# Moving half of the first pool half's window sums from the own blocks into attention's first units

## The chip, the cores and the metric

One Trainium2 chip, one program on all 8 cores. Each core owns 2,048 of the 16,384 positions and reads a halo of 2,048 positions before them; the cores do not talk to each other. The time of a run is device microseconds of its slowest core; a kernel's time is the median of its runs.

## The reference, cut to what matters

The layer runs a dilated window attention and a pooling mixer on one projection of the normalised input, merges them with gates, and follows with a SwiGLU network. The part that the change touches is the pooling mixer's trailing means:

```
for g, w in enumerate(POOL_WINDOWS):          # 2, 4, 8, 16; 64 channels each
    c = c0[:, :, g]                            # running sums of u
    ...
    z = (c[:, 1:] - lag) / cnt - ug[:, :, g]   # trailing mean minus the token
    outs.append(jnp.einsum('bsc,cd->bsd', z, w_mix[g]))
y = jnp.concatenate(outs, axis=-1) * scale
```

## The kernel before, in words

Every engine's program is written out in Python in the order in which that engine runs it; a semaphore wait stands ahead of an instruction that needs another engine's result. There is no planner: the place of a call in the code is its place in each engine's queue.

The program has five stages: the halo, the own blocks, attention, the merge with the gates and the output projection, and the feed-forward network. Two of them matter here.

**The own blocks** (loop over `b`, four blocks of 512 positions; inside it 12 chunks `n`). For each chunk TensorE makes a projection of q or k (eight matmuls, L449). In blocks 2 and 3 `rope_swap` turns it: VectorE multiplies the projection by the cosine and sine tables in one instruction (L548, out tile `t`), four small DMAs, two from SP's queue and two from ScalarE's, swap the rows of the sine part (`t2s<-t`), and GpSimd adds the two (L560). A projection lands in one of six PSUM banks and L548 sets the bank free. Four tiles `t` go round, so an L548 also waits for the L560 of four chunks earlier. After every third chunk a `u_unit` projects the pool's input and ScalarE copies it to `X` (L700).

The pool's 256 channels are two halves. The first half (`c0`, windows 2 and 4) is summed by `window_c0` in quarters of 512 positions, four VectorE pieces each: a pair sum (L721, `Y<-X`), a sum of pairs on the upper 64 partitions (L725, `Z<-Y`), and two means minus the token (L710, `zT<-Y` and `zT<-Z`, 64 partitions each). `c0_steps` is the list of these 16 pieces; before, one of them stands behind each of 16 consecutive L548, in the second half of block 2 and in block 3 up to chunk 9. The second half (`c1`, windows 8 and 16) is summed by `window_c1` in two halves of 1,024 positions, six pieces each (L732, L736, L739, L742, two L710).

**Attention** (loop over `u`, 48 units, group 2 in units 0 to 15, group 1 in 16 to 31, group 0 after them). In iteration `u` TensorE makes the scores of unit `u` (L852), projects v block `u`+3 (L569), and applies unit `u`-2 (L874, L879). ScalarE makes the exponential (L856, tile `PT`), copies the v block out of PSUM (L573) and, in group 2, copies the applied unit into `acc` (L894). VectorE multiplies by the mask (L861) and, from group 1 on, adds the applied unit to `acc` (L897). v blocks have two PSUM banks (6 and 7), and so have applied units (4 and 5, `o_ring`). Three v blocks are projected ahead of unit 0. In units 4, 8 and 12 VectorE copies the v block out in place of ScalarE (L575). At unit 1 VectorE's queue waits for the end of all rotary work (`ev_rope`, among it the last L560), at unit 2 ScalarE's. One `c1` piece stands in each of the units 1, 2, 3, 5, 6, 7, 9, 10, 11, 13, 14, 15. `pool_mix` (L811 on TensorE, L813 on ScalarE) maps the first half in units 17 to 20 and the second in 22 to 25. The first gate weights (`wgs`) are loaded once the last mean is there (`ev_wz[1]`) and used from unit 45 on.

Of the kernel before, what the change touches and what calls it, by code (L numbers as in the profile page):

```python
# [191 lines left out]
def build_program(taps=(), stop_after=None):  # L192
# [33 lines left out]
    pe, act, dve, pool, sp = P.pe, P.act, P.dve, P.pool, P.sp  # L226
# [251 lines left out]
    def k_dst(g, pr, e0, n):  # L478
        return kT[g][:, pr, e0 - KOFF[g]:e0 - KOFF[g] + n]
# [228 lines left out]
    def pool_mean(c, p0, S, X, t0, n, ev):  # L708
        p1 = p0 + 64
        ev = dve.op(lambda e: e.scalar_tensor_tensor(out=zT[p0:p1, c, t0:t0 + n], in0=S, scalar=invw[p0:p1, c:c + 1],  # L710
                                                     in1=X[p0:p1, t0 + 16:t0 + 16 + n], op0=ALU.mult, op1=ALU.subtract), waits=[ev])
        if t0 == 0:
            ev = dve.op(lambda e: e.tensor_tensor(out=S[:, 0:16], in0=S[:, 0:16], in1=invc[p0:p1, c, :], op=ALU.mult), waits=[ev])
            ev = dve.op(lambda e: e.tensor_tensor(out=zT[p0:p1, c, 0:16], in0=S[:, 0:16], in1=X[p0:p1, 16:32], op=ALU.subtract), waits=[ev])
        ev_wz[c] = ev

    def window_c0(q):
        X, t0, st = Xc[0], 512 * q, {}

        def y1():  # L720
            st[0] = dve.op(lambda e: e.tensor_tensor(out=Y0[:, :], in0=X[:, t0 + 14:t0 + 528], in1=X[:, t0 + 13:t0 + 527], op=ALU.add),  # L721
                           waits=ev_X[0] + [ev_wz[0], xst_free[2:4]])

        def z1():
            st[1] = dve.op(lambda e: e.tensor_tensor(out=Z0[64:128, :], in0=Y0[64:128, 2:514], in1=Y0[64:128, 0:512], op=ALU.add), waits=[st[0]])  # L725
        return [y1, z1, lambda: pool_mean(0, 0, Y0[0:64, 2:514], X, t0, 512, st[1]), lambda: pool_mean(0, 64, Z0[64:128, :], X, t0, 512, st[1])]

    def window_c1(hh):
        X, t0, st = Xc[1], 1024 * hh, {}

        def y1():
            st[0] = dve.op(lambda e: e.tensor_tensor(out=Y1[:, 1:LH], in0=X[:, t0 + 1:t0 + LH], in1=X[:, t0:t0 + LH - 1], op=ALU.add),  # L732
                           waits=ev_X[1] + [ev_wz[0], ev_wz[1]])

        def z1():
            st[1] = dve.op(lambda e: e.tensor_tensor(out=Z1[:, 3:LH], in0=Y1[:, 3:LH], in1=Y1[:, 1:LH - 2], op=ALU.add), waits=[st[0]])  # L736

        def y2():
            st[2] = dve.op(lambda e: e.tensor_tensor(out=Y1[:, 7:LH], in0=Z1[:, 7:LH], in1=Z1[:, 3:LH - 4], op=ALU.add), waits=[st[1]])  # L739

        def z2():
            st[3] = dve.op(lambda e: e.tensor_tensor(out=Z1[64:128, 15:LH], in0=Y1[64:128, 15:LH], in1=Y1[64:128, 7:LH - 8], op=ALU.add), waits=[st[2]])  # L742
        return [y1, z1, y2, z2, lambda: pool_mean(1, 0, Y1[0:64, 16:LH], X, t0, 1024, st[3]), lambda: pool_mean(1, 64, Z1[64:128, 16:LH], X, t0, 1024, st[3])]

    c0_steps = [f for q in range(4) for f in window_c0(q)]
    rope_ev = {}
    tick_at = {0: (1, 5, 7, 9), 1: (0, 2, 4, 6, 8, 9, 10)}
    for b in range(4):
        tab = tab_own
        order = (10, 11, 8, 9, 6, 7, 4, 5, 2, 3, 0, 1) if b < 3 else (10, 4, 11, 5, 8, 2, 9, 3, 6, 0, 7, 1)  # L750
        for n, c in enumerate(order):
            g = c // 2 if c < 6 else 0
            dst = q_dst(c, b) if c < 6 else k_dst(c // 2 - 3, c % 2, HT + b * 512, 512)
            ew = [wld_ev["w%s%d" % ("q" if c < 6 else "k", c // 2 % 3)], [hev[own + 4 * b + t] for t in range(4)]]
            if b < 2:
                rope_unit(c, hT[:, :, b * 512:(b + 1) * 512], 512, g, tab, dst, ew)
            else:
                rope_ev[c] = rope_swap(c, hT[:, :, b * 512:(b + 1) * 512], g, tab, dst, ew)
            if n == 0 and b < 3:
                tab_own = load_tables(b % 2, HT + (b + 1) * 512, 12)  # L760
            if n in tick_at.get(b, ()):
                own_tick(1)
            if b == 0 and n == 3:
                for pr in range(2):
                    k_halo(1, pr)
                    own_tick(1)
                for r in range(4):
                    v_halo(1, r, "dve")
                    if r == 1:
                        rope_flush()  # L770
                    if r % 2:
                        own_tick(1)
            if b == 0 and n == 5:
                for pr in range(2):
                    k_halo(0, pr)
                v_halo(0, 0, "dve")
                for c2 in range(2):
                    wload("wu", wu_t[c2][:, :, :], wu_d[c2])
            if b == 1 and n == 5:
                for c2 in range(2):  # L780
                    u_halo(c2)
                wload("masks", masks[:, :, :], masks_d[:, :, :])
                for g in range(4):
                    c, hf = g // 2, g % 2
                    wload("wmix", wmixb[64 * hf:64 * hf + 64, c, 64 * hf:64 * hf + 64], wmix_d[g, :, :], waits=[ev_ms4])
            if b == 1 and n == 11:
                act.wait(pe.last())
                dve.wait(pe.last(), act.last())
                for c2 in range(2):
                    ev_X[c2].append(dve.op(lambda e, c2=c2: e.tensor_copy(out=Xc[c2][:, 0:16], in_=uh[:, c2, :])))  # L790
            if b > 1 and n % 3 == 2:
                u_unit(b - 2, n // 3)
            if 0 <= 12 * (b - 2) + n - 6 < 16:
                c0_steps[12 * (b - 2) + n - 6]()
    assert own_k == [7, 15]
    ev_qk = pe.last()
# [3 lines left out]
    def v_own(g, s_, m, evac="act"):  # L800
        if g == 0:
            cols = slice((m - 1) * 128, m * 128)
        elif g == 1:
            cols = slice(512 * (m - 1) + s_, 512 * m, 4)
        else:
            cols = slice(s_, 2048, 16)
        v_block(wvr, g, lambda k: hT[:, k, cols], blk_idx(g, s_, m), evac=evac)

    def pool_mix(c, b):
        k_, bank, fr = pj_ring.get()  # L810
        ev = pe.op(lambda e: e.matmul(ps[:, bank, 0:512], lhsT=wmixb[:, c, :], rhs=zT[:, c, b * 512:(b + 1) * 512], start=True, stop=True),  # L811
                   waits=[fr, bank_free[bank], wld_ev["wmix"], ev_wz[c]])
        ev2 = act.op(lambda e: e.activation(out=ypool[:, c, b * 512:(b + 1) * 512], in_=ps[:, bank, 0:512], func=AF.Copy,  # L813
                                            scale=pscale[:, c:c + 1]), waits=[ev])
        pj_ring.release(k_, ev2)
        bank_free[bank] = ev2
# [107 lines left out]
    wgs = [P.sb("wgs%d" % i, [128, 2, 8, 128], BF16, R_ST + 8 * KB + i * 4 * KB) for i in range(2)]  # L924
    d_wm2 = P.dsem("d_wm2")
    d_wg = [P.dsem("d_wg%d" % i) for i in range(2)]
    c1_steps = dict(zip((1, 2, 3, 5, 6, 7, 9, 10, 11, 13, 14, 15), window_c1(0) + window_c1(1)))
    v_list = [(2, n, 1) for n in range(16)] + [(1, n // 4, 1 + n % 4) for n in range(16)] + [(0, 0, 1 + n) for n in range(16)]
    nv = 0
    napp = 0  # L930
# [9 lines left out]
    for u in range(-1, len(units) + 2):  # L940
        if u == 2:
            act.wait(*ev_rope)
        if 0 <= u < len(units):
            att_scores(u)
            if u == 15:
                ev_q2 = pe.last()
        while nv < min(len(v_list), u + 4):
            v_own(*v_list[nv], evac="dve" if u in (4, 8, 12) else "act")
            nv += 1
        if u == 1:  # L950
            dve.wait(*ev_rope)
        if 17 <= u < 21:
            pool_mix(0, u - 17)
        if u in c1_steps:
            c1_steps[u]()
        if 22 <= u < 26:
            pool_mix(1, u - 22)
            ev_yp = act.last()
        for _ in range({45: 3, 46: 3, 47: 3, 48: 4, 49: 3}.get(u, 0)):
            gate_mm()  # L960
        if napp <= u - 2:
            att_apply(napp)
            if napp == 15:
                ev_g2 = pe.last()
            napp += 1
        if u == 28:
            wg_ev = [pool.dma(wgs[i][:, :, :, :], wg_d[i], d_wg[i], waits=[ev_wz[1]]) for i in range(2)]
            pool.dma(wpa[:, :, :], wpa_d[:, :, :], d_wm2, waits=[ev_g2])
            ev_wp = pool.dma(wpp[:, :, :], wpp_d[:, :, :], d_wm2)
        if u in (38, 42, 47):  # L970
            norm_inv((u - 38) // 4)
        if u in (40, 44, 49):
            norm_mul((u - 40) // 4)
# [255 lines left out]
    for hf in range(2):  # L1229
# [39 lines left out]
        for il in range(8):  # L1269
            i = hf * 8 + il  # L1270
            b = i % 2
# [123 lines left out]
```

How the kernel before makes its waits and increments, by code:

```python
    def wait(self, *evs):  # L40
        for ev in evs:
            if ev is None:
                continue
            if isinstance(ev, (list, tuple)):
                self.wait(*ev)
                continue
            key = id(ev.sem)
            if self.seen.get(key, 0) >= ev.val:
                continue
            self.seen[key] = ev.val
            sem, val = ev.sem, ev.val
            self.meta.append(("wait", id(sem), val))
            self.ops.append(lambda e, sem=sem, val=val: e.wait_ge(sem, val))
# [1 line left out]
    def op(self, fn, waits=(), signal=True):  # L55
        self.wait(*waits)
        if signal:
            self.count += 1
            sem, val = self.sem, self.count
            self.meta.append(("inc", id(sem), 1))
            self.ops.append(lambda e, fn=fn, sem=sem: fn(e).then_inc(sem, 1))
            return Ev(sem, val)
        self.ops.append(lambda e, fn=fn: fn(e))
        return None
# [4 lines left out]
    def dma(self, out, in_, dsem, waits=(), **kw):  # L69
        self.wait(*waits)
        dsem.count += 16
        sem = dsem.sem
        self.meta.append(("inc", id(sem), 16))
        self.ops.append(lambda e, out=out, in_=in_, sem=sem, kw=kw: e.dma_start(out=out, in_=in_, **kw).then_inc(sem, 16))
        return Ev(sem, dsem.count)
```

## Time and profile before

| | |
|---|---|
| median of 3 runs | 983.3 us (982.0 to 983.87) |
| profiled execution | 982.04 us |
| its span, slowest core (core 6) | 980.5 us |
| spans of the eight cores | 975.4 to 980.5 us |
| TensorE busy | 916.5 us, 93% of the span |
| VectorE, ScalarE, GpSimd busy | 41%, 34%, 30% |

The span runs from the first to the last instruction of a core; the execution's own time is 1.5 us longer than the span of its slowest core. Times in the trace are microseconds from the span's start on core 6, if no other core is named. On core 6 the last projection of the own blocks ends at 197.9 us, attention runs to about 304 us, the merge and output projection and then the feed-forward network fill the rest.

### The profile page before, as it was taken

What the parts mean: (1) busy time and instruction counts of PE and PEld (TensorE: products, weight loads), DVE (VectorE), ACT (ScalarE), POOL (GpSimd) and SP (SyncE); (2) the same over time, 40 slices, a digit from 0 to 9 for tenths busy, and PEclk for the clock granted to TensorE, in tenths of its full rate; (3) what the DMA queues carried; (4) which work ended last, traced back from release to release, by engine and by line L of the source; (5) the groups of instructions that cost most, each with busy time, mean ns of one, the idle gap of its engine ahead of it and who ended that gap; (6) DMA issues with size and microseconds to landing.
All of it is one profiled execution on the core that took longest, in us unless ns stands there. A gap on an engine that the chain in (4) does not pass through costs nothing.

```text
span 980.5 us, 15129 instructions; the slowest of 8 cores (975.4 to 980.5 us)
## 1 busy us (share of the span) xinstructions
PE 916.5 (93%) x5422; PEld 461.2 (47%) x5508; DVE 406.5 (41%) x547; ACT 334.9 (34%) x576; POOL 290.3 (30%) x310
## 2 busy tenths in 40 slices
PE   3789999989999999999999999989999999999993
PEld 2455554457764444444544444444444444444441
DVE  3576787967876322323875111111112111121111
ACT  5675650069876222225661111110101111110110
POOL 3444685630001433324562111112231000001231
PEclk9899999999999999999999999999999999999997
DMA  9997324420501721208879666762324544430332
GB/s 244 272 239 194 108 46 118 110 53 6 84 2 43 110 42 22 44 1 216 297 205 174 118 112 114 117 110 65 129 94 120 87 67 84 71 59 20 110 120 74
DMA packets 37482, 105.45 MB, mean 108 GB/s; under 512 B 5792, under 2 KB 5792, under 8 KB 37408
## 3 DMA queue, kind: packets, MB, share of 16 engines
q0 software_dynamic: 15296, 42.05, 26.2%
q1 hardware_dynamic: 19664, 59.26, 18.5%
q10 hardware_dynamic: 2448, 3.18, 1.3%
q8 instruction: 45, 0.74, 0.3%
q14 instruction: 29, 0.24, 0.1%
HBM read 123.43 MB, written 16.78 MB: 143 GB/s over the span
## 4 chain that ended last, share of the span: by engine, by line
PE 82%; DVE 4%; issue 3%; ACT 3%; DMA 3%; POOL 3%; another core or an unknown queue 0%; ACTq 0%; SPq 0%; DVEq 0%; POOLq 0%
PE ps L1279 15%; PE ps L1245 15%; PE ps L1248 15%; PE ps L449 11%; PE ps L569 6%; PE ps L1019 5%; PE ps L1022 5%; POOL x1b L1095 2%; PE ps L874 2%; ACT junk L359 2%; PE ps L1026 1%; PE ps L852 1%; PE ps L1029 1%; DMA wvr<-wv 1%; PE ps L1082 1%
## 5 line engine op out<-in xcount | busy, mean ns | idle before, releaser
L1245 PE MATMUL ps<-hT,wgu 128*128 128x512 bf16 x659 | 157.6, 379 | 0.7
L1248 PE MATMUL ps<-hT,wgu 128*128 128x512 bf16 x658 | 157.4, 379 | 0.7
L1279 PE MATMUL ps<-wdn,ffT 128*128 128x512 bf16 x689 | 151.3, 379 | 3.1 <-DMA wdn<-wdn 2.3
L1260 DVE TENSOR_TENSOR ffT<-ps,sa 128x512 bf16<-128x512 f32 x88 | 60.8, 691 | 222.5 <-PE ps L1248 212.6
L1259 ACT ACTIVATE sa<-ps 128x512 f32<-128x512 f32 x88 | 52.5, 597 | 239.6 <-PE ps L1245 231.0
L1279 PEld LDWEIGHTS ps<-wdn,ffT 128*128 128x128 bf16 x704 | 68.8, 98 | 85.7 <-issue 2.8
L1248 PEld LDWEIGHTS ps<-hT,wgu 128*128 128x128 bf16 x672 | 65.8, 98 | 79.3
L1245 PEld LDWEIGHTS ps<-hT,wgu 128*128 128x128 bf16 x672 | 65.6, 98 | 78.7
L74 POOL DMA_DIRECT2D wgu<-wgu x42 | 22.6, 537 | 234.6 <-PE ps L1248 215.3
L1095 POOL TENSOR_TENSOR x1b<-tb,xin 128x1024 f32<-128x1024 f32 x31 | 72.8, 2348 | 55.1 <-DVE tb L1090 31.7
L449 PE MATMUL ps<-hT,wqk 128*128 128x512 bf16 x373 | 87.0, 381 | 0.9 <-issue 0.4
L1041 POOL TENSOR_TENSOR mT<-m,m 128x512 bf16<-128x512 f32 x32 | 40.6, 1269 | 151.3 <-DVE m L1036 151.3
L359 ACT ACTIVATE junk<-ps 128x1024 bf16<-128x1024 f32 x31 | 31.5, 1017 | 142.0 <-PE ps L1279 124.4
L1090 DVE SCALAR_TENSOR_TENSOR tb<-ps,rsA,gfin 128x1024 f32<-128x1024 f32 x15 | 19.3, 1284 | 131.5 <-POOL rsA L343 131.5
L1035 DVE TENSOR_TENSOR m<-ps,sga 128x512 f32<-128x512 f32 x32 | 22.1, 692 | 91.6 <-PE ps L1026 87.6
L1019 PE MATMUL ps<-hT,wgs 128*128 128x512 bf16 x242 | 58.3, 379 | 1.5 <-DVE m L1036 1.2
L569 PE MATMUL ps<-wvr,hT 128*128 128x256 bf16 x384 | 52.6, 282 | 6.0 <-DVE t L548 4.5
L1082 PE MATMUL ps<-wout,mT 128*128 128x512 bf16 x250 | 56.6, 379 | 1.7 <-DVE m L1036 1.4
L449 PEld LDWEIGHTS ps<-hT,wqk 128*128 128x128 bf16 x384 | 37.1, 98 | 43.2 <-issue 1.9
L1022 PE MATMUL ps<-hT,wgs 128*128 128x512 bf16 x241 | 57.1, 379 | 0.0
L856 ACT ACTIVATE PT<-ps 128x1024 bf16<-128x1024 f32 x48 | 53.3, 1111 | 9.0 <-PE ps L852 9.0
L569 PEld LDWEIGHTS ps<-wvr,hT 128*128 128x128 bf16 x384 | 38.7, 121 | 13.1 <-issue 7.2
(136 smaller groups left out, 1130.8 us busy)
## 6 DMA issues: line engine op xcount, KB each, us to landing
wgu<-wgu POOLq DMA_DIRECT2D x42, 512.0 KB, 6.4
xst<-xh SPq DMA_DIRECT2D x16, 512.0 KB, 19.7
xin<-xo SPq DMA_DIRECT2D x16, 512.0 KB, 6.7
x1s<-x1b SPq DMA_DIRECT2D x16, 512.0 KB, 4.6
xin<-x1s SPq DMA_DIRECT2D x16, 512.0 KB, 4.0
out<-x1b SPq DMA_DIRECT2D x15, 512.0 KB, 2.9
xst<-xo SPq DMA_DIRECT2D x12, 512.0 KB, 7.4
wdn<-wdn POOLq DMA_DIRECT2D x22, 256.0 KB, 7.5
```

The lines of the kernel that those rows point to most:

```text
L449: ev = pe.op(lambda e, k=k: e.matmul(ps[:, bank, 0:n], lhsT=wfn(k), rhs=rhsfn(k), start=(k == 0), stop=(k == 7)), signal=(k == 7))
L569: ev = pe.op(lambda e, k=k: e.matmul(ps[:, bank, 0:256], lhsT=tok_ap_fn(k), rhs=wv_tile[:, 2 - g, k, :], start=(k == 0), stop=(k == 7)), s ...
L856: ev_e = act.op(lambda e: e.activation(out=PT[k3][:, :, :], in_=ps[:, b0:b0 + 2, :], func=AF.Exp, scale=0.125), waits=[ev, pt_free[k3]])
L1019: e1 = pe.op(lambda e, k=k, wb=wb, b1=b1, tok=tok: e.matmul(ps[:, b1, :], lhsT=wgs[wb][:, 0, k, :], rhs=hT[:, k, tok], start=(k == 0), sto ...
L1022: e2 = pe.op(lambda e, k=k, wb=wb, b2=b2, tok=tok: e.matmul(ps[:, b2, :], lhsT=wgs[wb][:, 1, k, :], rhs=hT[:, k, tok], start=(k == 0), sto ...
L1082: ev = pe.op(lambda e, k=k, hf=hf, pr_=pr_: e.matmul(ps[:, pr_[0] + hf, :], lhsT=mT[:, k, i * 128:(i + 1) * 128], rhs=wout[:, k, hf * 512: ...
L1095: ev_o = pool.op(lambda e: e.tensor_tensor(out=outbuf[:, :], in0=tb[b][:, :], in1=xres[:, :], op=ALU.add), waits=[ev_t, ev_xres, out_free])
L1245: e1 = pe.op(lambda e, k=k, wbuf=wbuf, ba=ba, tok=tok: e.matmul(ps[:, ba, :], lhsT=wbuf[:, 0, k, :], rhs=hT[:, k, tok], start=(k == 0), st ...
L1248: e2 = pe.op(lambda e, k=k, wbuf=wbuf, bb=bb, tok=tok: e.matmul(ps[:, bb, :], lhsT=wbuf[:, 1, k, :], rhs=hT[:, k, tok], start=(k == 0), st ...
L1259: es = act.op(lambda e, ub=ub, ba=ba: e.activation(out=sa[ub][:, :], in_=ps[:, ba, :], func=AF.Silu), waits=[e1, sa_free[ub]])
L1260: ef = dve.op(lambda e, ub=ub, bb=bb, j=j, b=b: e.tensor_tensor(out=ffT[:, j, b * 512:(b + 1) * 512], in0=ps[:, bb, :], in1=sa[ub][:, :], ...
L1279: ev = pe.op(lambda e, j=j, h2=h2, pr_=pr_, il=il: e.matmul(ps[:, pr_[0] + h2, :], lhsT=ffT[:, j, il * 128:(il + 1) * 128], rhs=wdn[:, j, ...
```

## The change

The first eight `c0` pieces stay where they were. The other eight (the third and fourth quarter) leave block 3 and come, two at a time, in attention's units 1 to 4. The `c1` pieces move from units 1 to 15 to units 5 to 24, `pool_mix` of the second half from units 22 to 25 to units 27 to 30, the call that loads the gate weights from unit 28 to 32, and v block 7 (unit 4) is copied out by ScalarE in place of VectorE.

```diff
-            if 0 <= 12 * (b - 2) + n - 6 < 16:
+            if 0 <= 12 * (b - 2) + n - 6 < 8:
                 c0_steps[12 * (b - 2) + n - 6]()
...
-    c1_steps = dict(zip((1, 2, 3, 5, 6, 7, 9, 10, 11, 13, 14, 15), window_c1(0) + window_c1(1)))
+    c1_steps = dict(zip((5, 6, 7, 9, 10, 11, 13, 14, 15, 18, 21, 24), window_c1(0) + window_c1(1)))
...
-            v_own(*v_list[nv], evac="dve" if u in (4, 8, 12) else "act")
+            v_own(*v_list[nv], evac="dve" if u in (8, 12) else "act")
             nv += 1
         if u == 1:
             dve.wait(*ev_rope)
+        if 1 <= u < 5:
+            for f in c0_steps[6 + 2 * u:8 + 2 * u]:
+                f()
         if 17 <= u < 21:
             pool_mix(0, u - 17)
         if u in c1_steps:
             c1_steps[u]()
-        if 22 <= u < 26:
-            pool_mix(1, u - 22)
+        if 27 <= u < 31:
+            pool_mix(1, u - 27)
...
-        if u == 28:
+        if u == 32:
             wg_ev = [pool.dma(wgs[i][:, :, :, :], wg_d[i], d_wg[i], waits=[ev_wz[1]]) for i in range(2)]
```

VectorE's queue at the end of block 3, before; the rows run from chunk 6's L548 to the first mask of attention (`t` is the turned projection, `ps` a PSUM bank, `cs` the tables):

```order
 L548 TENSOR_TENSOR t_2_56_98<-ps,cs_44_86 128x1024
 L721 TENSOR_TENSOR Y_66_108<-X_62_104 128x514
 L548 TENSOR_TENSOR t_3_57_99<-ps,cs_44_86 128x1024
 L725 TENSOR_TENSOR Z_67_109<-Y_66_108 64x512
 L548 TENSOR_TENSOR t_0_54_96<-ps,cs_44_86 128x1024
 L710 SCALAR_TENSOR_TENSOR zT_110<-Y_66_108,cpk_47,X_62_104 64x512
 L548 TENSOR_TENSOR t_1_55_97<-ps,cs_44_86 128x1024
 L710 SCALAR_TENSOR_TENSOR zT_110<-Z_67_109,cpk_47,X_62_104 64x512
 L548 TENSOR_TENSOR t_2_56_98<-ps,cs_44_86 128x1024
 L548 TENSOR_TENSOR t_3_57_99<-ps,cs_44_86 128x1024
 L861 TENSOR_TENSOR PT_72_114<-PT_72_114,masks_45 128x1024
```

These four pieces, and the four of the quarter ahead of them, are gone from the queue between the L548. VectorE's queue of the changed kernel in units 0 to 4 (L861 is the mask of a unit):

```order
 L861 TENSOR_TENSOR PT_72_114<-PT_72_114,masks_45 128x1024
 L861 TENSOR_TENSOR PT_70_112<-PT_70_112,masks_45 128x1024
 L721 TENSOR_TENSOR Y_66_108<-X_62_104 128x514
 L725 TENSOR_TENSOR Z_67_109<-Y_66_108 64x512
 L861 TENSOR_TENSOR PT_71_113<-PT_71_113,masks_45 128x1024
 L710 SCALAR_TENSOR_TENSOR zT_110<-Y_66_108,cpk_47,X_62_104 64x512
 L710 SCALAR_TENSOR_TENSOR zT_110<-Z_67_109,cpk_47,X_62_104 64x512
 L861 TENSOR_TENSOR PT_72_114<-PT_72_114,masks_45 128x1024
```

In units 3 and 4 the same four pieces follow for the last quarter. The last three `c1` pieces now fall among group 1's additions; VectorE's queue of the changed kernel around unit 24:

```order
 L861 TENSOR_TENSOR PT_71_113<-PT_71_113,masks_45 128x1024
 L897 TENSOR_TENSOR acc_111<-ps,acc_111 128x2x256
 L861 TENSOR_TENSOR PT_73_115<-PT_73_115,masks_45 128x1024
 L710 SCALAR_TENSOR_TENSOR zT_110<-Z_65_107,cpk_47,X_63_105 64x1024
 L897 TENSOR_TENSOR acc_111<-ps,acc_111 128x2x256
```

The mean (L710) stands ahead of an L897; before, no pool piece stood behind unit 15.

## Rows read from the trace of the kernel before

**Rows 1.** Section 1 of the page: TensorE's busy time, share and instructions.

```profile
PE 916.5 (93%) x5422; PEld 461.2 (47%) x5508; DVE 406.5 (41%) x547; ACT 334.9 (34%) x576; POOL 290.3 (30%) x310
```

**Rows 2.** Span of the slowest core, with its mean granted clock.

```profile
core 6: 980.5 us, clock 0.986
```

**Rows 3.** TensorE's waits from 100 to 215 us (total us, times, longest).

```profile
PE ps L569 <- DVE t L548: 4.5, 1, 4.5
```

**Rows 4.** TensorE's timeline around the stage's end: start, us, instruction, idle before.

```profile
190.82 5.36 PE L449 MATMUL ps<-hT,wqk 128*128 128x512 bf16 x24
196.02 1.89 PE L449 MATMUL ps<-hT,wu 128*128 128x512 bf16 x8
202.37 3.56 PE L569 MATMUL ps<-wvr,hT 128*128 128x256 bf16 x16 [4.46 <-DVE t L548]
206.13 1.07 PE L569 MATMUL ps<-wvr,hT 128*128 128x256 bf16 x8 [0.20 <-ACT vA L573]
...
208.56 0.46 PE L852 MATMUL ps<-qT,kT 64*128 64x128 bf16 x8
```

**Rows 5.** Busy time by stretch; the number behind POOL's is the granted clock.

```profile
202.40:204.00 1.60, 1.60 (x8) 1.28 (x9) 0.95 (x1) 0.00 (x0) 1.28 (x1) 0.50 0.31 78
```

**Rows 6.** VectorE's groups from 181.2 to 201 us: busy, mean ns.

```profile
L725 DVE TENSOR_TENSOR Z<-Y 64x512 f32<-64x512 f32 x2 | 3.9, 1930 | 0.1
L710 DVE SCALAR_TENSOR_TENSOR zT<-Y,cpk,X 64x512 bf16<-64x512 f32 x2 | 3.6, 1776 | 0.0
L710 DVE SCALAR_TENSOR_TENSOR zT<-Z,cpk,X 64x512 bf16<-64x512 f32 x2 | 2.8, 1382 | 0.1
L721 DVE TENSOR_TENSOR Y<-X 128x514 f32<-128x514 f32 x2 | 1.4, 684 | 0.0
```

**Rows 7.** VectorE's timeline in the own blocks.

```profile
162.15 0.69 DVE L725 TENSOR_TENSOR Z<-Y 64x512 f32<-64x512 f32 x1
...
177.41 0.73 DVE L710 SCALAR_TENSOR_TENSOR zT<-Y,cpk,X 64x512 bf16<-64x512 f32 x1
...
200.99 2.36 DVE L548 TENSOR_TENSOR t<-ps,cs 128x1024 f32<-128x1024 f32 x2
```

**Rows 8.** GpSimd's last instruction of the own blocks.

```profile
206.59 1.28 POOL L560 TENSOR_TENSOR qT<-t,t2s 128x512 bf16<-128x512 f32 x1
```

**Rows 9.** ScalarE's timeline: the first v copies, then exponentials of units 3 to 5.

```profile
205.61 0.80 ACT L573 ACTIVATE vA<-ps 128x256 bf16<-128x256 f32 x2
...
213.43 1.12 ACT L856 ACTIVATE PT<-ps 128x1024 bf16<-128x1024 f32 x1
...
215.53 1.14 ACT L856 ACTIVATE PT<-ps 128x1024 bf16<-128x1024 f32 x1
...
217.31 1.15 ACT L856 ACTIVATE PT<-ps 128x1024 bf16<-128x1024 f32 x1
```

**Rows 10.** VectorE's timeline in attention: units 1 to 3.

```profile
211.92 1.23 DVE L732 TENSOR_TENSOR Y<-X 128x1039 f32<-128x1039 f32 x1
213.07 0.69 DVE L861 TENSOR_TENSOR PT<-PT,masks 128x1024 bf16<-128x1024 bf16 x1
213.67 1.24 DVE L736 TENSOR_TENSOR Z<-Y 128x1037 f32<-128x1037 f32 x1
```

**Rows 11.** TensorE's timeline in attention: scores of units 3 and 4, application of unit 2.

```profile
212.15 0.47 PE L852 MATMUL ps<-qT,kT 64*128 64x128 bf16 x8
...
214.13 0.47 PE L852 MATMUL ps<-qT,kT 64*128 64x128 bf16 x8
...
215.56 0.41 PE L874 MATMUL ps<-PT,vA 128*64 128x128 bf16 x8
```

**Rows 12.** TensorE's waits from 205 to 310 us.

```profile
PE ps L569 <- ACT vA L573: 1.2, 3, 0.6
```

**Rows 13.** VectorE's timeline in group 1: addition of unit 19, mask of unit 22.

```profile
252.09 1.11 DVE L897 TENSOR_TENSOR acc<-ps,acc 128x512 f32<-128x512 f32 x1
253.39 0.69 DVE L861 TENSOR_TENSOR PT<-PT,masks 128x1024 bf16<-128x1024 bf16 x1 [0.19 <-ACT PT L856]
```

## The prediction

> **What bounds the kernel now.** I read the page first. TensorE is busy 93% of the span [rows 1], so a change to VectorE's work can gain only where TensorE stands still, and every pause is worth its own length. Next the waits of TensorE, stretch by stretch. Between 100 and 215 us there is one large wait: the first v block of attention waits 4.5 us for an L548 [rows 3]. TensorE's timeline shows the place: the last projection ends at 196.02 + 1.89 = 197.91, the next matmul starts at 202.37 [rows 4]. Then the clock: after that pause the granted clock is 0.50, the 1.2 GHz level [rows 5], and the first two v blocks take 3.56 us where the third, at full clock, takes 1.07 [rows 4]. So the join of the two stages costs the 4.46 us pause and 3.56 - 2 x 1.03 = 1.5 us of slow matmuls.
>
> Why is L548 late? A projection tile takes (196.02 - 190.82) / 3 = 1.73 us on TensorE [rows 4]. The last tile that VectorE must turn is done one tile before the end, at 197.91 - 1.73 = 196.2, but the last two L548 run from 200.99 to 203.35 [rows 7]: VectorE is 5.9 us behind. In its last 20 us it ran eight pool pieces, 3.9 + 3.6 + 2.8 + 1.4 = 11.7 us [rows 6]. These are the pieces that leave.
>
> **The change, part by part, on core 6, the slowest [rows 2].**
>
> *Eight pieces leave block 3.* VectorE loses 11.7 us of work ahead of a point at which it is 5.9 us late, so it has 5.8 us to spare and is then paced by TensorE: the last L548 starts at 196.2 + 0.15 and ends at 197.55 (1.18 apiece, 2.36 for two [rows 7]), 5.8 us earlier than 203.35. The ring of four `t` tiles could hold it back: an L548 waits for the L560 four chunks before. From the last L548's end, 203.35, to the last L560's end, 206.59 + 1.28 = 207.87 [rows 8], is 4.5 us, and four chunks last at least 4 x 1.73 = 6.9 us, which leaves 5.7 between the one L548's end and the other's start; no wait.
>
> TensorE then runs v blocks 0 and 1 without pause, 2 x 1.03, to 199.97. v block 2 needs ScalarE's copy of block 0, which stands behind the last L548's DMA issues in ScalarE's queue. In the row it starts at 206.13, 2.78 after the last L548's end [rows 4, 7, 9]; now 197.55 + 2.78 = 200.33. TensorE stands 0.36 us there, too little for anything that the rows show the clock to do. All behind it moves by 206.13 - 200.33 = **5.8 us**. This holds the pause and the slow matmuls together; they are not added again.
>
> *The pieces arrive in units 1 to 4, two each.* No row shows them in attention. From below: 0.68 for L721 [rows 6], 0.69 for L725 and 0.73 for each L710 [rows 7], the shortest rows, 5.7 us for eight. From above: the 11.7 us that they took in block 3. I take the low end, because the rows nearest in place are the `c1` pieces at the same spot, 1.23 and 1.24 us for twice the length [rows 10], without spread, while GpSimd, which adds alongside in block 3, is done at 207.87 [rows 8]; now, 5.8 us earlier, at about 202, ahead of unit 1's pieces, which come where the `c1` piece stood, at 211.92 - 5.8 = 206.1 [rows 10]. A unit's mask takes 0.60 start to start [rows 10], so VectorE has 0.60 + 0.69 + 0.69 (or 2 x 0.73) = 2.0 to 2.1 us of work in a unit of 214.13 - 212.15 = 1.98 us [rows 11]. It falls back by up to 0.1 a unit, 0.4 in all. Mask of unit 2 ends at 213.76 [rows 10] and is used at 215.56 [rows 11]: 1.8 us to spare. TensorE does not wait: **0**. That cover is gone if the pieces keep block 3's price (a rival below).
>
> Block 3 shows the spread itself: L725 takes 0.69 once [rows 7] and 1.93 on average while L560 run [rows 6], and L548, with one input in PSUM, stays at 1.18. The Trainium skill ("SBUF — State Buffer", section "Who interferes with whom") says that a VectorE instruction with two SBUF inputs and a GpSimd instruction that reads SBUF shut each other out for a whole instruction. By that rule the pieces cost 5.7 us in attention, and the sum stays; by block 3's averages they cost 11.7 and some 4 us of the gain are lost.
>
> *v block 7's copy goes to ScalarE.* Its exponentials start 2.10 us apart with the copy, 1.78 without [rows 9]: 0.3 us more in group 2, where 2.10 exceeds TensorE's 1.98. TensorE already waits 1.2 us for ScalarE's v copies in attention [rows 12], so the loss arrives: **+0.3**. Its bound below is 0, if unit 4's lead absorbs it.
>
> *`c1` pieces move.* Units 5 to 15 hold nine at the old price and spacing; nothing there. The last three stand in units 18, 21 and 24, each ahead of an addition. VectorE's spare time there is 0.19 a unit [rows 13], against 1.24 a piece [rows 10]: behind by 3 x 1.24 - 6 x 0.19 = 2.6 us after unit 24. An addition must end before the application two units on, since there are two banks: 2 x 1.98 - 0.41 - 1.11 = 2.4 us of slack [rows 11, 13]. TensorE waits 0.2; with the 0.2 us pool matmul gone from each of units 22 to 25, which lets TensorE come sooner, up to 0.9. I take **+0.6**; bounds 0 and 1.5.
>
> *`pool_mix` and the gate weights.* The four pool matmuls come five units later, none added: 0. The gate weights' load waits for the last mean, now in unit 24; they are needed in unit 45, 21 units of over 1.9 us on, some 40 us: 0.
>
> **Sum:** -5.8 + 0.3 + 0.6 = -4.9 us. The profiled execution took 982.04, its span 980.5; it would take 977.1. It lies 1.26 below the median of 983.3, so the median becomes **978.4 us**.
>
> **The rivals.**
>
> 1. *The pieces keep block 3's price.* 11.7 / 8 = 1.46 each: 0.60 + 2.9 = 3.5 us of VectorE in a unit of 1.98, 6.1 us behind after four units, less 1.8 spare: TensorE waits 4.3. Then -4.9 + 4.3 = -0.6: 982.7, no change. For it: only the averages. Against it: GpSimd is idle there, and the `c1` rows have no spread.
>
> 2. *Slower: the pause moves into attention and takes the clock along.* Place: application of units 2 to 4, behind VectorE's queue. If each piece took 1.85, the mean of the two dearest groups of block 3 (1.93 and 1.78 [rows 6]), a pair takes 3.7; four units hold 4 x (0.60 + 3.7) = 17.2 us against 7.9: 9.3 behind, 7.5 us of waiting after the slack, and 1.5 us of slow matmuls as after today's pause. Sum -4.9 + 9.0 = +4.1: 987.4. It decides once a pair costs over 1.38 + (4.9 + 1.8) / 4 = 3.1 us. That needs GpSimd's L560 beside units 1 to 4; VectorE's queue waits at unit 1 for the last L560, so the pieces can't meet one.
>
> 3. *A smaller gain.* The catch-up in block 3 is slowed by the DMAs between L548 and L560, or group 1's additions cost their bound: 2 us less, 980.4.
>
> **How the numbers follow.** About 0.2%, 2 us, is what a measurement of this kernel can tell from no change. The forecast has 0.78. Its join gives between 6.0 (the pause and the slow matmuls whole, if ScalarE comes in time) and 5.0 (the last L548 0.8 late), attention takes back between 0 and 0.3 + 1.5: 977.3 to 980.1. Rival 3 has 0.10, faster too (980.4 is 2.9 below 983.3). Rival 1 has 0.08, the same; rival 2 has 0.04, slower. So 0.88, 0.08, 0.04. The runs before lie between 982.0 and 983.87, some 1 us to either side of the median; that widens the ends, and the range 975.8 to 981.0 holds the forecast and rival 3.
>
> **What would show it.** TensorE's wait for L548 gone or under 0.5 us; the granted clock 1.00 from 196 to 208; scores of unit 1 near 202.8 in place of 208.56; the last L548 ending within 2 us of the last projection's start. L721, L725 and L710 of units 1 to 4 at 0.7 us each. A short wait of L874 near unit 26. The merge starting 4.5 to 5.5 us earlier, with everything after it unchanged. Wrong would be: L548 still late (then something other than the pieces holds VectorE), pieces at 1.4 us in attention with waits of L874 in units 2 to 6, or a clock of 0.50 anywhere past 197 us.

## The result and the profile after

| | before | changed |
|---|---|---|
| median of 8 runs | 983.59 us | 977.28 us |
| ratio, 95% interval | | 0.9943 [0.9933, 0.9953] |
| profiled execution | 982.04 us | 976.32 us |
| span of its slowest core | 980.5 us (core 6) | 974.8 us (core 5) |

The medians hold every run, also three slow ones of over 1,000 us (two before, one changed), which the ratio leaves out. The ratio makes 5.6 us of 983.59, between 4.6 and 6.6: faster, as forecast. The forecast was 978.4 with a range of 975.8 to 981.0. A second series of the same kernel, beside the last experiments below, gave 0.9944 [0.993, 0.9958].

TensorE's busy time, section 1 of the page of the changed kernel, answers to [rows 1]; its share rises from 93% to 94%:

```profile
PE 920.7 (94%) x5508; PEld 459.8 (47%) x5508; DVE 400.1 (41%) x546; ACT 334.8 (34%) x577; POOL 288.9 (30%) x310
```

(The longer busy time goes with 86 more recorded matmuls; the number of weight loads is 5508 in both.) TensorE's timeline at the join of the two stages, core 5 of the changed kernel, answers to [rows 4]:

```profile
197.30 1.89 PE L449 MATMUL ps<-hT,wu 128*128 128x512 bf16 x8
199.03 1.91 PE L569 MATMUL ps<-wvr,hT 128*128 128x256 bf16 x16
201.35 1.07 PE L569 MATMUL ps<-wvr,hT 128*128 128x256 bf16 x8 [0.41 <-ACT vA L573]
...
203.78 0.46 PE L852 MATMUL ps<-qT,kT 64*128 64x128 bf16 x8
```

The pause of 4.46 us is gone: v block 0 starts as the last projection ends. The first two v blocks take 1.91 us in place of 3.56. What is left is v block 2's wait for ScalarE, 0.41 us. The clock in the stretch of [rows 5] is 1.00 now, the 2.4 GHz level (the number behind POOL's):

```profile
202.40:204.00 1.60, 1.60 (x23) 1.33 (x24) 0.00 (x0) 1.47 (x2) 0.84 (x1) 1.00 0.04 10
```

VectorE's timeline at the end of block 3 shows why; it answers to [rows 7]:

```profile
184.24 1.23 DVE L548 TENSOR_TENSOR t<-ps,cs 128x1024 f32<-128x1024 f32 x1 [0.40 <-POOL kT L560]
186.16 2.46 DVE L548 TENSOR_TENSOR t<-ps,cs 128x1024 f32<-128x1024 f32 x2 [0.70 <-POOL qT L560]
189.30 1.22 DVE L548 TENSOR_TENSOR t<-ps,cs 128x1024 f32<-128x1024 f32 x1 [0.69 <-POOL qT L560]
...
197.64 1.22 DVE L548 TENSOR_TENSOR t<-ps,cs 128x1024 f32<-128x1024 f32 x1 [0.50 <-PE ps L449]
```

VectorE catches up by 191 us. On the way it waits three times for GpSimd, which the prediction had excluded; after that it waits for TensorE, and the last L548 ends 0.17 us before the last projection does. The moved pieces in units 1 to 4 (VectorE's groups from 206 to 216 us: count, busy, mean ns) have the low price, 0.69 to 0.75 us, where block 3 took 1.46 on average [rows 6]. There, on core 6 of the kernel before, the two L721 took 0.7 us and the six other pieces 1.14 to 2.42 us; each of the six lies beside an L560 of GpSimd and ends 0.54 to 0.56 us after an L560 has ended (the first L725 runs from 183.09 to 185.51, and the L560 in whose time it starts ends at 184.95). In units 1 to 4 there is no L560 left:

```profile
L710 DVE SCALAR_TENSOR_TENSOR zT<-Z,cpk,X 64x512 bf16<-64x512 f32 x2 | 1.5, 750 | 0.1
L710 DVE SCALAR_TENSOR_TENSOR zT<-Y,cpk,X 64x512 bf16<-64x512 f32 x2 | 1.5, 739 | 0.0
L725 DVE TENSOR_TENSOR Z<-Y 64x512 f32<-64x512 f32 x2 | 1.4, 690 | 0.2
L721 DVE TENSOR_TENSOR Y<-X 128x514 f32<-128x514 f32 x2 | 1.4, 687 | 0.0
```

TensorE's waits from 180 to 320 us of the changed kernel, core 5, answer to [rows 3, 12]:

```profile
PE ps L569 <- ACT vA L573: 1.4, 3, 0.6
...
PE ps L874 <- DVE acc L897: 0.7, 3, 0.4
PE ps L569 <- DVE vA L575: 0.7, 1, 0.7
```

For the experiments I cut the span of every core in four: up to the end of the last projection (start of the last `wu` group plus 1.73 us), from there to the scores of unit 1 (the **join**), from there to the merge's first matmul on `oT` (**attention**), and the rest. Means over the eight cores of one profiled execution, in us:

| kernel | own blocks | join | attention | rest | span |
|---|---|---|---|---|---|
| before | 195.8 | 10.91 | 95.60 | 675.6 | 977.9 |
| changed | 196.6 | 4.81 | 96.53 | 674.6 | 972.5 |
| changed, second series | 196.6 | 4.84 | 96.49 | 674.6 | 972.6 |

The join is 6.1 us shorter and attention 0.9 longer: 5.2 us. The two other parts differ by 0.8 and 1.0 us with opposite signs, and vary by 1.6 to 4.5 us from core to core in each kernel; no part of the change lies in the rest, and from the own blocks it only takes work away.

### The profile page after: what moved, and what is told of

It is laid out like the page before. It is cut to its first block, busy times and chain, and to the rows that moved or that the text cites. A ratio compares the mean times of both kernels' runs of the same rounds, so it can differ in the third digit from the quotient of the medians.

```text
span 974.8 us, 15215 instructions; the slowest of 8 cores (970.3 to 974.8 us)
## 1 busy us (share of the span) xinstructions
PE 920.7 (94%) x5508; PEld 459.8 (47%) x5508; DVE 400.1 (41%) x546; ACT 334.8 (34%) x577; POOL 288.9 (30%) x310
## 4 chain that ended last, share of the span: by engine, by line
PE 84%; DVE 3%; ACT 3%; DMA 3%; POOL 2%; issue 2%; ACTq 0%; SPq 0%; DVEq 0%; POOLq 0%
PE ps L1282 16%; PE ps L1248 15%; PE ps L1251 15%; PE ps L449 12%; PE ps L569 6%; PE ps L1022 6%; PE ps L1025 5%; POOL x1b L1098 2%; PE ps L874 2%; PE ps L852 2%; ACT junk L359 2%; PE ps L1029 1%; PE ps L1032 1%; DMA wvr<-wv 1%; DMA xst<-xh 1%
## 5 line engine op out<-in xcount | busy, mean ns | idle before, releaser
L341 POOL TENSOR_SCALAR msA<-ssA 128x1 f32<-128x1 f32 x36 | 7.8, 215 | 126.9 <-ACT junk L359 101.3
```

## The experiments

The edits of e4 are against the kernel before, all others against the changed kernel. The theory: what makes VectorE late at the end of block 3 is the pool pieces among its last L548; taking them away closes the pause, and attention has room for them. The rivals: the gain comes from the later second half; it comes in proportion to the pieces; it comes from the clock; attention has any amount of room.

**The rest of the change without the move (e1).**

```diff
-            if 0 <= 12 * (b - 2) + n - 6 < 8:
+            if 0 <= 12 * (b - 2) + n - 6 < 16:
...
-        if 1 <= u < 5:
-            for f in c0_steps[6 + 2 * u:8 + 2 * u]:
-                f()
```

> All 16 first-half pieces stay in the own blocks; the rest of the change (second half's pieces, its pool maps, v block 7's copy by ScalarE, the weight load's place) is kept. Theory (the eight pieces ahead of the last L548 make VectorE late, and only their leaving gains): the wait of L569 for L548 stays at 2.5 to 5 us on every core, the slow clock behind it stays, scores of unit 1 come 10 to 11.5 us after the last projection; attention pays its 0.3 to 0.9 us; 0 to 1 us slower than before. Rival (the later second-half pieces relieve attention, and the gain lies there): the pause stays, but attention is shorter, 2 us or more faster than before.

Measured: 0.9997 [0.9988, 1.0006]; join 10.46 (9.3 to 11.4 over the cores, where 10 to 11.5 was expected), attention 96.52. TensorE's waits on its slowest core, 180 to 320 us:

```profile
PE ps L569 <- DVE t L548: 4.6, 1, 4.6
...
PE ps L874 <- DVE acc L897: 0.7, 3, 0.4
PE ps L569 <- DVE vA L575: 0.7, 1, 0.7
```

The pause stays, and attention pays the same 0.9 us as in the changed kernel. So the rest of the change gains nothing and costs 0.9 us of attention, of which the time shows nothing (0.3 us faster, between 1.2 faster and 0.6 slower); all of the gain is the move's. The moved pieces themselves cost attention nothing: 96.52 without them, 96.53 and 96.49 with them.

**Half of the move (e2).**

```diff
-            if 0 <= 12 * (b - 2) + n - 6 < 8:
+            if 0 <= 12 * (b - 2) + n - 6 < 12:
...
-        if 1 <= u < 5:
-            for f in c0_steps[6 + 2 * u:8 + 2 * u]:
+        if 1 <= u < 3:
+            for f in c0_steps[10 + 2 * u:12 + 2 * u]:
```

> As the change, but only the last quarter's four pieces leave block 3 (units 1 and 2 hold them); the third quarter's four stay. Theory (5.9 us late, and each quarter took 4.9 to 6.8 us in block 3): four pieces less leave VectorE 0 to 1 us late, so the pause is under 1.2 us, no slow clock, and the time is within 1 us of the change's: 4.6 to 6.5 us faster than before. Rival (gain in proportion to the pieces that leave): half of it, 2.5 to 3.2 us faster, with a pause of 2 us or more.

Measured: 0.9979 [0.9968, 0.999], 2.1 us faster. The theory's number is refuted; the proportional rival is nearer, though the gain is below its range too (the interval, 1.0 to 3.1 us, reaches it). By pieces left in block 3 the join is 10.46 (eight), 7.57 (four) and 4.84 (none). The single cores differ: 5.6 to 5.9 us on three of them, 7.9 to 9.5 on five. TensorE's timeline on the slowest core:

```profile
199.24 1.04 PE L569 MATMUL ps<-wvr,hT 128*128 128x256 bf16 x8
201.96 1.07 PE L569 MATMUL ps<-wvr,hT 128*128 128x256 bf16 x8 [1.69 <-DVE t L548]
204.42 1.90 PE L569 MATMUL ps<-wvr,hT 128*128 128x256 bf16 x8 [1.39 <-ACT vA L573]
```

and VectorE's last two L548 there:

```profile
197.31 1.22 DVE L548 TENSOR_TENSOR t<-ps,cs 128x1024 f32<-128x1024 f32 x1 [0.71 <-POOL kT L560]
200.59 1.23 DVE L548 TENSOR_TENSOR t<-ps,cs 128x1024 f32<-128x1024 f32 x1 [2.06 <-POOL qT L560]
```

Four pieces less do let VectorE catch up, but in a burst, and then the next link holds it: the last L548 waits 2.06 us for the L560 four chunks earlier, since there are four tiles `t` and GpSimd and the DMAs between work through the burst at their own pace. So lateness is not only VectorE's own backlog; GpSimd's chain inherits it. (In the kernel before, no L548 of these last chunks waits for an L560.) With all eight gone the same waits fall at 183 to 189 us and are over in time. On this core the clock falls as well, after two pauses of which neither lasts 2 us. From the last L548's end to the scores of unit 1 it takes 6.88 us here and 5.03 on the same core of the changed kernel; so of the 4.6 us by which the join is longer than there, 2.7 are the later L548 and 1.9 the slow clock behind it. Four of the eight cores lose 1.2 to 1.9 us to the clock in this way. Two stretches of this core (TensorE's busy time stands first behind the length, the clock behind POOL's):

```profile
201.00:203.00 2.00, 1.04 (x8) 0.87 (x8) 0.82 (x1) 0.00 (x0) 2.00 (x3) 1.00 0.01 2
...
205.00:207.00 2.00, 2.00 (x16) 1.22 (x15) 0.00 (x0) 0.40 (x2) 1.18 (x1) 0.50 0.00 0
```

**The moved pieces twice (e3).** The outputs stay what they were, the pieces only run twice, each after the one ahead of it.

```diff
-            for f in c0_steps[6 + 2 * u:8 + 2 * u]:
+            for f in 2 * c0_steps[6 + 2 * u:8 + 2 * u]:
+                dve.wait(dve.last())
                 f()
```

> As the change, with the two pieces of each of units 1 to 4 issued twice, so that a unit's pair costs VectorE about 3.0 us in place of 1.5; what rival 1 and 2 of the prediction spoke of, a pair at twice its price. Theory (VectorE falls behind by what a unit's work exceeds TensorE's 1.98 us, and 1.8 us of slack is all there is): 4 x (0.6 + 3.0 - 1.98) = 6.5 us behind, waits of L874 of 4 to 5.5 us in units 2 to 7; the gain almost gone, 0 to 2 us faster than before. Rival (masks have so much lead that VectorE's queue is off the path): no wait of L874 there, 5 us or more faster, as the change.

Measured: 1.0018 [1.0009, 1.0027], 1.8 us slower than before, where 0 to 2 us faster was expected; join 4.81, attention 104.8 (104.0 to 105.3 on seven cores; 107.8 on the slowest, core 0, with a single pause of 2.1 us more that was not looked into). TensorE's waits on that core, then stretches of its attention:

```profile
PE ps L874 <- DVE PT L861: 4.4, 4, 2.1
```

```profile
208.00:212.00 4.00, 2.95 (x36) 2.20 (x35) 3.55 (x6) 4.00 (x7) 0.00 (x0) 1.00 0.00 0
...
216.00:220.00 4.00, 2.75 (x26) 1.90 (x26) 3.55 (x6) 1.94 (x4) 0.00 (x0) 0.50 0.00 0
220.00:224.00 4.00, 3.38 (x30) 2.12 (x28) 3.97 (x5) 2.18 (x4) 0.00 (x0) 0.50 0.00 0
```

The waits are the 4 to 5.5 us expected (4.2 to 5.8 over the cores, in the four units 2 to 5), so the slack of VectorE's queue was sized right, and the rival that it is off the path falls. But attention grew by 8.3 us: beside the waits the clock fell to 0.50 for some 10 us, which the expectation left out. This is rival 2 of the prediction made real: at a unit's price of 3.1 to 3.3 us (the four pieces from 205.38 to the next mask at 208.49, on the slowest core) the change would lose.

**The pause filled, pieces where they were (e4).** Sixteen matmuls whose results nothing reads, in the kernel before.

```diff
+    for _ in range(16):
+        pe.op(lambda e: e.matmul(ps[:, 0, :], lhsT=ident[:, :], rhs=hT[:, 0, 0:512], start=True, stop=True), waits=[bank_free[0]], signal=False)
     for u in range(-1, len(units) + 2):
```

> The kernel before, with 16 matmuls of 512 columns (3.45 us, results unused) between the last projection and attention's first v block, so that TensorE does not stand still there; VectorE is as late as before. Reading A (the slow matmuls behind the pause cost 1.5 us on top of it): the clock stays at 1.00, the first v blocks take 1.03 us each, and the kernel is 1 to 1.5 us faster than before. Reading B (v block 2 waits for ScalarE's copy of block 0, which follows the last L548's DMA issues whatever the clock): the clock stays up but v block 2 starts as late as before, within 0.5 us of before.

Measured: 0.9999 [0.999, 1.0009]; join 10.40 us against 10.91 before. TensorE's timeline on the slowest core (core 3), and one stretch:

```profile
196.75 3.62 PE L941 MATMUL ps<-hT,ident 128*128 128x512 bf16 x16
201.70 2.20 PE L569 MATMUL ps<-wvr,hT 128*128 128x256 bf16 x16 [1.33 <-DVE t L548]
205.31 1.07 PE L569 MATMUL ps<-wvr,hT 128*128 128x256 bf16 x8 [1.42 <-ACT vA L573]
```

```profile
203.00:205.00 2.00, 0.89 (x8) 0.66 (x6) 0.00 (x0) 0.71 (x2) 0.50 (x2) 1.00 0.68 213
```

The clock holds at 1.00 there and the first two v blocks take 2.20 us, not 3.41 as on this core of the kernel before, yet v block 2 stands 1.42 us for ScalarE, and the time is the same. Reading B holds: v block 2 starts 2.62 to 2.79 us after the last L548's end on seven of the eight cores, and 2.62 to 2.78 us on seven cores of the kernel before, whatever the clock. (On core 6 of e4 it stood 2.24 us for ScalarE, and there the clock fell.)

But ScalarE's chain covers only the first two v blocks. In the kernel before, the pause was 2.5 to 2.9 us on five cores (0, 1, 2, 4 and 5), shorter than core 6's 4.46, and there the clock was still low behind it: v block 2 and the next take 1.9 us each, not 1.1. Core 0 of the kernel before:

```profile
202.35 1.90 PE L569 MATMUL ps<-wvr,hT 128*128 128x256 bf16 x8 [0.74 <-ACT vA L573]
204.18 0.66 PE L852 MATMUL ps<-qT,kT 64*128 64x128 bf16 x8
204.77 1.90 PE L569 MATMUL ps<-wvr,hT 128*128 128x256 bf16 x8
```

From the last L548's end to the scores of unit 1 it takes 6.9 to 7.0 us on these five cores and 5.9 on core 7, but 5.05 and 5.2 on cores 3 and 6, the two slowest, and 5.0 to 5.2 on seven cores of e4. So the slow matmuls cost the two slowest cores nothing and five others 1.8 to 1.9 us. The kernel's time, which is its slowest core's, shows none of that within 1 us.

**v block 7's copy back on VectorE (e5).**

```diff
-            v_own(*v_list[nv], evac="dve" if u in (8, 12) else "act")
+            v_own(*v_list[nv], evac="dve" if u in (4, 8, 12) else "act")
```

> As the change, but v block 7 (unit 4) is copied out by VectorE again. Theory (ScalarE is the tighter engine in group 2, so one copy more costs 0.3 us): waits of L569 for ScalarE around units 17 and 18 shrink by about 0.3 us and attention is 0.3 us shorter than in the change. Rival (VectorE is the later of the two in unit 4, so its copy comes late): a new wait of L569 for L575 of 0.2 to 0.5 us around unit 6 takes the place, attention the same within 0.1 us or longer.

Measured: 0.9944 [0.9932, 0.9956], as the change. TensorE's waits:

```profile
PE ps L569 <- ACT vA L573: 1.5, 3, 0.6
...
PE ps L569 <- DVE vA L575: 0.6, 2, 0.3
```

The waits for ScalarE are no shorter; the wait of 0.7 us for VectorE's copy becomes two of 0.3. On seven of the eight cores attention is 96.36 to 96.51, about 0.1 us shorter at most than the change's 96.49. The eighth had a single wait of 1.3 us more at a pool map, not looked into. The rival is nearer: where the copy runs moves a wait and hardly changes the sum.

**The first three copies on VectorE (e6).** It stands idle there; a wait for the L560 that still reads the place keeps order.

```diff
     act.wait(sw_free[:2])
+    dve.wait(sw_free[0])
...
-            v_own(*v_list[nv], evac="dve" if u in (8, 12) else "act")
+            v_own(*v_list[nv], evac="dve" if u in (-1, 8, 12) else "act")
```

> As the change, but VectorE copies out the first three v blocks, ahead of unit 0, where it stands idle. Theory (v block 2 waits 0.4 to 0.55 us for ScalarE, whose copy of block 0 stands behind the last L548's DMA issues): this wait goes, gap to scores of unit 1 4.2 to 4.5 us, 0.4 to 0.8 us faster than the change. Rival (the first exponential's table load holds unit 0 anyway, and ScalarE's later lag takes the gain back): the gap shrinks, but the waits for ScalarE around unit 17 grow by as much; the same as the change.

Measured: 0.992 [0.9908, 0.9933], a median of 975.58 beside 978.34 for the change in the same series. The join is 4.13 on every core, 0.7 us shorter, and attention is 96.63: the wait is gone and not given back. The medians differ by 2.8 us, more than the 0.4 to 0.8 expected and the 0.6 that these two parts explain; where the rest comes from is open, and the intervals of the two ratios overlap at their ends.

**Pieces and pool maps placed anew (e7).** On top of e6:

```diff
-    c1_steps = dict(zip((5, 6, 7, 9, 10, 11, 13, 14, 15, 18, 21, 24), window_c1(0) + window_c1(1)))
+    c1_steps = dict(zip((5, 6, 7, 9, 10, 11, 13, 14, 15, 16, 17, 20), window_c1(0) + window_c1(1)))
...
-        if 17 <= u < 21:
-            pool_mix(0, u - 17)
+        if 20 <= u < 24:
+            pool_mix(0, u - 20)
```

> As the run with the first three copies on VectorE, and besides: the last three pieces of the second half in units 16, 17 and 20 in place of 18, 21 and 24, and the first half's pool maps in units 20 to 23 in place of 17 to 20. Theory (the pool maps' copies meet ScalarE's last L894 in units 17 and 18, 1.0 us of waits, and the pieces of units 21 and 24 delay the additions, 0.35 us): both waits go; 1.5 to 2.5 us faster than the change, 7 to 8.5 us faster than before. Rival (waits only move: the additions wait instead): no more than 0.8 us faster than the change.

Measured: 0.9913 [0.9901, 0.9926], 8.6 us faster than before, a median of 975.18 and so not told apart from e6's 975.58; join 4.14, attention 95.05, so 2.1 us less than the change in these two parts. The ratios put it 3.0 us below the change, above the 1.5 to 2.5 expected; here too the rest is open. All of TensorE's waits on its slowest core (e6's edit puts the lines of attention and the merge one lower, so L875 is L874 above):

```profile
PE ps L1023 <- DVE m L1040: 1.2, 1, 1.2
PE ps L569 <- DVE vA L575: 0.7, 1, 0.7
PE ps L875 <- DVE acc L898: 0.4, 2, 0.2
```

The waits for ScalarE's copies are gone, and so is the addition's of 0.35 us near unit 26. Two things were moved at once here, so which of them removed which wait is read from the places and not shown by the run. The 0.7 us behind the copy of unit 12 stays. (The first row is the merge's, in every kernel.)

## Why the prediction was right, point by point

- *The eight pieces cause the pause, and their leaving closes it.* Right: e1 keeps everything else and gains nothing; join 10.46 with them, 4.84 without.
- *The join gains 5.8 us.* On core 6, for which it was worked out, the join goes from 10.81 to 4.87 us, 5.9: the last L548 ends 5.8 us earlier, set against the end of the last projection, and the chain behind it is 0.2 shorter. Over the cores the gain is 6.1, but made up otherwise: 4.7 are the earlier L548, since most cores were less late than core 6, and 1.4 lie behind it, mostly the slow matmuls of the six cores named under e4. That 5.8 fits the mean as well is in part luck. v block 2's wait was foreseen at 0.36 and measured 0.41 on the slowest core. The 0.15 us from a tile's end to its L548 stands in no row; the last L548 of the changed kernel starts 0.34 us after its tile's end (197.64 against 197.30) and ends 0.17 us ahead of the last projection, not 0.36.
- *The pause "and 1.5 us of slow matmuls".* The description in the first part counted two losses; the sum went by the chain from the last L548 through ScalarE to v block 2 and counted one. e4 shows that the sum was right for the slowest cores, where the clock costs nothing behind ScalarE's chain. On five other cores the clock cost 1.8 to 1.9 us on top, so for them the description was nearer; the prediction read only core 6.
- *"5.8 us to spare", "no wait" in the ring of four tiles.* Wrong as a general step. The ring does hold the catch-up back (0.40, 0.70 and 0.69 us in the changed kernel, 2.06 on the slowest core of e2), so moving half of the pieces brings 2.1 us and not nearly all, the slow clock behind it adding its share. With the eight gone, VectorE was not paced by TensorE at once, as the step had it. It did no harm because the waits end at 189.3, some ten microseconds before the stage does. Rival 3 named this slowing, at 2 us; it cost nothing here.
- *The pieces cost 0.69 to 0.73 us each in attention, and TensorE does not wait.* Right: 0.69 to 0.75, attention the same with and without them. The Trainium skill ("SBUF — State Buffer", section "Who interferes with whom") has VectorE instructions with two SBUF inputs shut out by GpSimd instructions that read SBUF; the trace agrees, 1.46 us on average beside L560 [rows 6] and 0.7 with GpSimd done. Rival 1 is excluded by the rows, rival 2 by the same; that a unit's pieces at 3.1 to 3.3 us do make the kernel slower, as rival 2's threshold of 3.1 has it, e3 shows.
- *VectorE falls back by up to 0.1 us a unit there.* It took 2.15 us a unit (masks at 208.65, 210.81, 212.93 and 215.10), so 0.17: the second sum, which needs the first, starts 0.79 us after it and not 0.69, and each of the two means takes 0.77 to 0.78 from start to start and not 0.73. The slack covered it.
- *+0.3 for ScalarE's extra copy, +0.6 for the late pieces.* The sum of 0.9 was measured as 0.9, its parts not. The addition waits 0.35 us more, at the place named. ScalarE's waits did not grow, and taking the copy back gains about 0.1 at most (e5). The 1.2 us of rows 12, from which the +0.3 was argued, had been misread: 0.20 of it is the join's, and the two other waits (0.58 and 0.46 us, at 243.35 and 245.97) stand among the first half's pool maps, which take their banks from the same two as the v blocks; e7, where these maps come later, is without them. What was missed is VectorE's copy at unit 12, which now stands behind the two first means in units 10 and 11, as unit 8's did before behind units 6 and 7: 0.7 us of waiting against 0.3. Why the same neighbours cost 0.4 more there was not tried. So the step that every added copy on ScalarE reaches TensorE failed, and that the sum is met all the same is luck.

So the profiles give -5.9 + 0.7 = -5.2 on core 6 (attention from 95.80 to 96.49) and -6.1 + 0.9 = -5.2 over the cores, against -4.9 forecast, and the ratio gives -5.6 [-6.6, -4.6]; the differences lie within the interval.

## What to carry to other kernels

When TensorE pauses at the join of two stages, look at what the late engine ran in its last 20 us, and move what nobody waits for soon, to a place where the engines that shut it out are idle. Before crediting a clock drop with a loss, ask which chain ends last behind the pause, on every core: here ScalarE's DMA issues and copy covered the slow matmuls on the two slowest cores, and not on five others, whose pause was shorter. And lateness is passed on: clearing half of one engine's backlog only shows the ring behind it.

## What was not expected of the hardware

TensorE's clock fell to 0.50 after a single pause of 2.51 us (core 1 of the kernel before, where the next two v blocks took 2.73 us and the third 1.90) and after two pauses of 1.69 and 1.39 us with one v block between (e2, slowest core), while in e4 pauses of 1.33 and 1.42 us, after 16 matmuls that filled the time, left it at 1.00 (core 3). In e3 two waits of 0.43 and 2.08 us between matmuls of attention stood ahead of its fall at about 215 us, two more of 1.25 and 0.62 us came while it was down, and it was back some 10 us after the fall. No rule is drawn from these cases.
